# Two hand-kept instruction orders rewritten, and one gate load moved to another place in GpSimd's queue

## The reference

```
# block 1, per layer (adaLN scales from cond @ ada_w)
h = rmsnorm(x) * (1 + sc_m) + sh_m
proj = h @ w_in                       # 1024 -> 2824
out_a = sliding_window_attention(rope(norm(aq)), rope(norm(ak)), av)
out_b = rmsnorm(hgrn2_chunked(bq, log_f, bv)) * silu(bg)
out_c = rmsnorm(gated_delta_chunked(l2norm(cq), l2norm(ck), cv, beta, g)) * silu(cg)
x = x + gt_m * (concat(out_a, out_b, out_c) @ w_out)
x = x + gt_f * swiglu(rmsnorm(x) * (1 + sc_f) + sh_f)
# block 2, per layer
proj = x @ w_in_2                     # z, xbc, dt, dq, dk, dv, dg, cq, cg, gates
y_ssd  = ssd(forward + backward) * silu(z), rmsnorm
y_diff = rmsnorm(diff_attention(dq, dk, dv)) * silu(dg)
y_cross = attention(cq, mem @ w_mem_kv) * silu(cg)
merged = sum(gate_i * (y_i @ w_br_i))
x = layernorm(alpha * x + merged @ w_out_2)
```

## Time and profile before

| | |
|---|---|
| median of 3 runs | 3927.32 us (3926.3 to 3929.07) |
| the profiled execution | 3926.3 us, span 3923.8 us |
| TensorE busy | 3772.4 us, 96% of the span |
| VectorE busy | 2615.8 us, 67% |
| ScalarE busy | 1563.3 us, 40% |
| GpSimd busy | 181.5 us, 5% |
| granted TensorE clock, mean | 0.981 of full |

### The profile page before, as it was taken

One profiled execution on the slowest core, in us unless ns is written; L12 is line 12 of the kernel. 1 busy time (PEld: TensorE's weight loads), 2 busy tenths in 40 slices (PEclk: granted clock), 3 DMA queues, 4 the chain that ended last, 5 costly groups with the idle time before them and its releaser, 6 DMA issues.

```text
span 3923.8 us, 49406 instructions
## 1 busy us (share of the span) xinstructions
PE 3772.4 (96%) x19461; PEld 3094.3 (79%) x19461; DVE 2615.8 (67%) x4153; ACT 1563.3 (40%) x2633; POOL 181.5 (5%) x335
## 2 busy tenths in 40 slices
PE   7989999999999999999999999999999999999998
PEld 6769878888779788878887788678778877886786
DVE  6887455555785522457889753876668898437866
ACT  3453332234643422333443333554344433335542
POOL 0000000000000000000111000000001110000010
PEclk9999899999999899999999999999999999999999
DMA  7502256533212332334555232133244553331242
GB/s 239 181 22 76 81 169 211 190 115 97 68 39 65 111 97 83 105 113 132 157 164 161 70 99 81 63 120 132 74 152 141 156 169 97 92 91 60 71 151 106
DMA packets 226871, 451.59 MB, mean 115 GB/s; under 512 B 18560, under 2 KB 63648, under 8 KB 224592
## 3 DMA queue, kind: packets, MB, share of 16 engines
q1 hardware_dynamic: 197584, 335.12, 26.8%
q0 software_dynamic: 29056, 113.32, 9.1%
HBM read 412.45 MB, written 35.93 MB: 114 GB/s over the span
## 4 chain that ended last, share of the span: by engine, by line
PE 76%; DVE 15%; ACT 5%; DMA 2%; issue 2%; SPq 0%; DVEq 0%; POOL 0%; ACTq 0%; POOLq 0%
PE ps L605 59%; PE ps L148 11%; DVE arena L170 4%; PE ps L159 3%; DVE spl L170 3%; ACT arena L244 3%; DVE arena L185 3%; DVE sm L191 1%; PE ps L154 1%; DVE X L170 1%; ACT sph L244 1%; PE ps L900 1%; DVE arena L177 1%; DMA arena<-cumd 1%; DVE arena L221 1%
## 5 line engine op out<-in xcount | busy, mean ns | idle before, releaser
L170 DVE TENSOR_TENSOR spl<-ring,sph 128x1024 fp32r<-128x1024 f32 (+3 forms) x556 | 650.2, 1177 | 701.1 <-ACT sph L244 700.3
L244 ACT ACTIVATE sph<-ring 128x1024 fp32r<-128x1024 f32 (+3 forms) x556 | 558.7, 1019 | 723.7 <-PE ps L605 680.8
L605 PE MATMUL ps<-sph,HTh 128*128 128x512 f32 (+2 forms) x1632 | 636.0, 390 | 9.7 <-DVE HTl L170 5.0
L605 PE MATMUL ps<-spl,HTh 128*128 128x512 f32 (+2 forms) x1632 | 601.5, 369 | 0.0
L605 PE MATMUL ps<-sph,HTl 128*128 128x512 f32 (+2 forms) x1632 | 600.7, 368 | 0.0
L244 ACT ACTIVATE arena<-ps 128x512 f32<-128x512 f32 (+2 forms) x572 | 315.2, 563 | 675.1 <-PE ps L605 400.3
L605 PE MATMUL ps<-HTh,sph 128*128 128x512 f32 x1360 | 536.4, 394 | 0.3 <-DVE arena L170 0.3
L605 PE MATMUL ps<-HTh,spl 128*128 128x512 f32 x1360 | 529.6, 389 | 0.0
L605 PE MATMUL ps<-HTl,sph 128*128 128x512 f32 x1360 | 529.5, 389 | 0.0
L605 PE MATMUL ps<-sph 128*128 128x512 f32 x992 | 399.1, 402 | 4.8 <-DVE spl L170 4.8
L605 PE MATMUL ps<-sph,spl 128*128 128x512 f32 x992 | 389.0, 392 | 0.0
(11 more groups left out here) (228 smaller groups left out, 4919.5 us busy)
## 6 DMA issues: line engine op xcount, KB each, us to landing
ring<-in_w_in SPq DMA_DIRECT2D x264, 512.0 KB, 4.0
arena<-in_ada_w SPq DMA_DIRECT2D x88, 512.0 KB, 4.9
arena<-cumd POOLq DMA_DIRECT2D x128, 256.0 KB, 4.0
ring<-in_w_down SPq DMA_DIRECT2D x44, 512.0 KB, 3.7
ring<-in_w_gate SPq DMA_DIRECT2D x40, 512.0 KB, 3.8
ring<-in_w_up SPq DMA_DIRECT2D x40, 512.0 KB, 4.2
ring<-in_w_mem SPq DMA_DIRECT2D x32, 512.0 KB, 3.5
ring<-in_w_out SPq DMA_DIRECT2D x32, 512.0 KB, 3.7
```

What stands on the lines that cost most here:

```text
L170: self.e.tensor_tensor(o, a, b, op).then_inc(*self.done.up())
L244: self.e.activation(o, a, f, **kw).then_inc(*self.done.up())
L605: ins = pe.e.matmul(o, l, r, start=k0 == 0 and i == 0 and not b.pairs, stop=k0 + b.ks == b.kt and i == 3 * b.ks - 1 and (c0 > 0 or not b.p ...
```

## The change

The strings of ('mix', 0) and ('mix', 1) are replaced. Each has the same number of each letter as before, in another order; the strings of `proj` stay. And the load of gate half 1 goes from `pool_before` into `dnorm_pool`, to the first step of dnorm's second half, beside that of half 0 in the first.

```
 SCORES = {
     ('mix', 0):
-        "7MtMt5MtMt2Mt10M2a7Ma6MaMhMa5Mh2Mch2Mh2Mc4Mc5Mac3Ma7Mta3Mah4Ma7MaMa3McaMhca2Mh2Mhac4Mc2Mac2ga2gh3gah"
-        "gagagagag2agagagag2agag3a2g2agag2a2gmhgihihi2mihiMhMihiMihMihiMh2Mi2Mihihi2Mi4Mi2Mi2h3M2iMh2i2MhihMi"
-        "hMi2MhiMh2ihMih2Mh3MiM2iM2i2M3i2M2i3Mb22M",
+        "14Mt3MtM2t10MtM2a7Ma4Ma2MhMaMc2Mh3MhMh2Mc2Mc5Ma3Mca9Ma3Mah8Ma3Mc2MaMaMahMc2MaMahMc2Mc4Mc2gaha2gh3gah"
+        "a2gagagag2agagagag2agag2ag3a3g2a3gahmihtimhim2Mihi3MihiMi5M2hihi2Mih3MiMh2iM2iMihiMih2iMi2h2Mi2MhMihi"
+        "hMhihMh2iMihMh4MiM2iM2i2M2iMiM2i4Mb21M",
     ('mix', 1):
-        "26MaM3a5Ma2MhMhMa2M2aMa2M2ahaM2caMac7Mh4Mh5McMac2Ma2MaMa2MahcMaMhMhaMcMc2Mc2M3gh4gahga2ga2gaga2g2aga"
-        "gagag3agag3a3gmgih2i2mhi2MiMiMhMhiMhihiMh2MihM2ihihiM2ih3MihihMh3M2iMh3MhMiMhihiMiM2ihiMihMhi2M2iMih"
-        "i2M2i2MiM2iMb28M",
+        "24Ma7Ma2M2aMh2Ma2c2MhacMacM3aMhMhM3a2Ma7Mh4Mc4Mhac2MaMa3Maca2McMaMaMchMh4M2gh5gha2gag2a4gag2agag2aga"
+        "g2ag2ag2agm3gihimhim3Mhi2Mi2MhiMhihiMiMhihi3MiMhiMiMihMiMhi2h2MhMi3MhiMh2iM3ihihihiMhi2hMi2M2iM2i2M2"
+        "i2MiMiMi11Mb17M",
@@ def pool_before(p):
                 if which == 1:
-                    p.wait_ge(at["ds", l, 31, 1], *[at["stg", l, 28 + m] for m in range(4)])
-                    at["dgin", l, 1] = p.move(ld["dg"], DGb[1], Dg[:, :, 512:1024].rearrange("m p n -> p m n"))
                     p.wait_ge(at[("br", l, 0), "merged", 7], at[(("br", l, 0), 1), 3], *[at["stg", l, 32 + j] for j in range(8)])
                     at["cgin", l] = p.move(ld["cg"], OC, Cg.rearrange("m p n -> p m n"))
@@ def dnorm_pool(p, l):
             for nb in range(2):
+                p.wait_ge(at["ds", l, 16 * nb + 15, 1], *[at["stg", l, 24 + 4 * nb + m] for m in range(4)])
+                at["dgin", l, nb] = p.move(ld["dg"], DGb[nb], Dg[:, :, nb * 512:(nb + 1) * 512].rearrange("m p n -> p m n"))
                 if nb == 0:
-                    p.wait_ge(at["ds", l, 15, 1], *[at["stg", l, 24 + m] for m in range(4)])
-                    at["dgin", l, 0] = p.move(ld["dg"], DGb[0], Dg[:, :, 0:512].rearrange("m p n -> p m n"))
                     p.wait_ge(at["od_t", l, 15], at["mk_stored", l])
                     at["mkin", l] = p.move(ld["mk"], MK, KVd[l, :, 0:2048].rearrange("p (a b) -> p a b", a=4))
```

More of the change, by code:

```diff
@@ L46 @@
     ('mix', 0):
-        "7MtMt5MtMt2Mt10M2a7Ma6MaMhMa5Mh2Mch2Mh2Mc4Mc5Mac3Ma7Mta3Mah4Ma7MaMa3McaMhca2Mh2Mhac4Mc2Mac2ga2gh3gah"
-        "gagagagag2agagagag2agag3a2g2agag2a2gmhgihihi2mihiMhMihiMihMihiMh2Mi2Mihihi2Mi4Mi2Mi2h3M2iMh2i2MhihMi"
-        "hMi2MhiMh2ihMih2Mh3MiM2iM2i2M3i2M2i3Mb22M",
+        "14Mt3MtM2t10MtM2a7Ma4Ma2MhMaMc2Mh3MhMh2Mc2Mc5Ma3Mca9Ma3Mah8Ma3Mc2MaMaMahMc2MaMahMc2Mc4Mc2gaha2gh3gah"
+        "a2gagagag2agagagag2agag2ag3a3g2a3gahmihtimhim2Mihi3MihMi5M2hihi2Mih3MiMh2iM2iMihiMih2iMi2h2Mi2MhMihi"
+        "hMhihMh2iMihMh4MiM2iM2i2M2iMiM2i4Mb21M",
     ('mix', 1):
-        "26MaM3a5Ma2MhMhMa2M2aMa2M2ahaM2caMac7Mh4Mh5McMac2Ma2MaMa2MahcMaMhMhaMcMc2Mc2M3gh4gahga2ga2gaga2g2aga"
-        "gagag3agag3a3gmgih2i2mhi2MiMiMhMhiMhihiMh2MihM2ihihiM2ih3MihihMh3M2iMh3MhMiMhihiMiM2ihiMihMhi2M2iMih"
-        "i2M2i2MiM2iMb28M",
+        "24Ma7Ma2M2aMh2Ma2c2MhacMacM3aMhMhM3a2Ma7Mh4Mc4Mhac2MaMa3Maca2McMaMaMchMh4M2gh5gha2gag2a4gag2agag2aga"
+        "g2ag2ag2agm3gihimhim3Mhi2Mi2MhiMhihiMiMhihi3MiMhiMiMihMiMhi2h2MhMi3MhiMh2iM3ihihihiMhi2hMi2M2iM2i2M2"
+        "i2MiMiMi11Mb17M",
     ('proj', 0):
```

## The result

The changed kernel takes 3950.68 us (median of 4 runs, 3947.94 to 3954.68) against 3927.86 us, a ratio of 1.0064, 95% interval 1.0049 to 1.0080. It is slower by 23 us. The forecast was 3928.5 us, no change, with 3940 as the upper end of its range, and 0.16 for slower. It was wrong.

A forecast was written before the change was run, and what follows sets the result against it. TensorE, busy 3772.4 of 3923.8 us, was taken as the bound. Orders -2 -1 -1 -1.5 and load +4.2 +2.5 gave +1.2 on 3926.3, so 3927.5; with 1.0 for the median 3928.5 us, range 3915 to 3940.

The forecast's parts named there:

- Layer 1, first stretch: Stretch of mix layer 1 with projections: earlier convolution steps change the time by -1 us, between -2.6 and +1.
- the one that lost: Rival: eight close inverse steps in layer 1's third stretch wait 1.2 us each, 13 us more, about 3941 us; chance 0.14.
- The moved load: Last layer: half 1 lands late, VectorE waits 4.6 us, TensorE stops 4.2 us; hidden in layer 0, 0 for kvd.
- the term of 6.7: The load's share of the sum: 4.2 us of TensorE stop and 2.5 us of reduced clock in the last layer.
- The rival that the load is hidden: Half 1 lands before VectorE needs it in the last layer, only the orders count: 3921.8 us; chance 0.1.
- the estimate of 14.0 us: Time for 5.24 MB in one row by the skill page's figures, putting half 1's landing in the last layer just in time.
- The clock behind a stall: Reduced TensorE clock after the last layer's 4.2 us stop: 2.5 us lost, between 0 and 3.4.
- The other orders: New order in layer 0's first stretch -2 us, second stretches -1 (layer 0) and -1.5 (layer 1), third and fourth 0.
- second to fourth stretches of layer 1: mix layer 1 without main steps (-1.5 us), inverse with memory products (0), serial state pass (0).
- the wait of 6.16 us: TensorE's wait for VectorE in layer 0's first stretch, inside one h step; forecast to stay.
- the 7.03 us: TensorE's wait for VectorE at g11 in layer 1's second stretch; forecast to fall to about 5.
- its inputs are long ready: Claim that a24, 3.68 us long, placed before g11 in layer 1's second stretch, can run in TensorE's idle time there.

The follow-up runs named there:

- conv_only: The kernel before with only four convolution steps, c0 to c3 of mix layer 1, moved earlier: 3940.01 us, +12.7.
- h3_early: The kernel before with one step moved, h3 (decayed linear attention) of mix layer 1, seven main steps earlier: 3936.74 us, +6.7.
- front_old: The kernel before with the new string of mix layer 1 only from the first g step on: 3930.84 us against 3930.03.
- load_only: The kernel before with only the load of gate half 1 moved, both strings old: 3934.51 us against 3927.27.
- orders_only: The changed kernel with the load of gate half 1 back in its old place, both new strings kept: 3944.11 us, +16.8.
- mix1_only: The kernel before with only the string of mix layer 1 replaced by the new one: 3943.05 us, +15.8.
- load_mid: The kernel before with the load of gate half 1 issued between those of kvd and the four gd tiles: 3928.26 us against 3927.55.
- h3_c5: The kernel before with two steps of mix layer 1 moved earlier, h3 directly behind main step 41 and c5 behind c4: ratio 1.0017.

## Why the prediction was wrong, step by step

**The failed step is "Layer 1, first stretch".** It took -1 us, between -2.6 and +1, and the stretch lost 12.4. I bounded the gain by a row, TensorE's 2.6 us of idle time, and the loss by nothing: "may hold VectorE a little" has no row behind it. I looked at c3 and asked whether its own data would be there. The question that decides is who stands behind it. VectorE is busy 89.70 of 110 us there, the c steps are 10.5 us of work with no hurry, and moved up they stand ahead of a softmax and of low parts that TensorE waits for. The rows for it were in the trace of before. a8 came 11.9 us later against the opening product, and 10.5 for c0 to c3 and 2.9 for a4 (no longer done in an earlier idle time of VectorE), less VectorE's 0.77 and 0.60 us of idle time there, make 12.0. conv_only and h3_early show that such a move alone costs TensorE 8.2 and 4.2 us. None of the rivals had it: the one that lost put its loss into the close run i18 to i25, where front_old shows nothing.

**The moved load** was right in its mechanism and nearly in its size. Alone it has 4.63, 4.03 and about 1.7 us for the forecast's 4.6, 4.2 and 2.5, and +7.2 us for the term of 6.7. Half 1 landed 17.9 us after the issue of `cgd`, for the 18.6 worked out; that the wait of VectorE still came out at 4.6 is luck, for VectorE too was there 0.7 us sooner after that issue (13.3 us for 14.0). In layer 0 it was hidden, as forecast: no wait for it is in the trace. Nor was anything won for `kvd` in layer 0, where TensorE waits 2.35 us for 2.44. In the changed kernel the same load costs about 8 us, because half 1 landed 1.6 us later there; whether the orders have to do with that is open. The rival that the load is hidden, and with it the estimate of 14.0 us by the page "DMA: Bandwidth & Descriptors" of the Trainium skill (Anatomy of one DMA), is refuted: 17.9 and 19.5 us were measured, beside a weight load on another queue.

**The clock behind a stall.** Between 0 and 3.4 us was the range, 2.5 taken; 1.7 was read in load_only, and about 16 x 0.21 = 3.4 us in the changed kernel, whose window from 3768 to 3784 has 0.79:

```profile
3768.00:3784.00 16.00, 10.37 (x40) 8.38 (x39) 10.65 (x20) 0.00 (x0) 0.00 (x0) 0.79 0.01 4
```

The page "TensorE: Matmul & The Clock Gate" of the Trainium skill (HAM oscillation) says that waits for data re-throttle the array each time; both windows agree, with 0.86 and 0.79. The full 3.4 us that the prediction worked out with it came in the second and not in the first.

**The other orders.** For layer 0 and for the second to fourth stretches of layer 1 I counted -2, -1, -1.5 and 0. Measured are 1 us (orders_only less mix1_only) and 0.8 (front_old less the kernel before), both within noise. That they are near nothing was right; the gains of 4.5 us in all are not there to see. In layer 0 the wait of 6.16 us of the earlier trace rows is 6.72 in the changed kernel. In layer 1 the 7.03 us did not shrink in the way that was forecast. a24 does stand ahead of g11 now, but it can't run at once there, as "its inputs are long ready" had it: TensorE waits 3.95 us for VectorE in front of it, and again in front of the g steps, 0.56, 1.47 and 1.02 us, 7.0 us in all. TensorE of front_old:

```profile
1079.01 3.51 PE L148 MATMUL ps<-arena 128*64 128x512 f32 x4 [3.95 <-DVE arena L185]
```

What follows starts within 1 us of where it did, for VectorE's chain sets the end, as the prediction itself had said.

**The range** had 3940 as its upper end because every term that could lose had a bound of a few microseconds. One missing bound made it 11 us too narrow.

## What to carry to other kernels

Before a step is moved up in an in-order schedule, add up its work on each engine and ask for every instruction that it is put ahead of who needs that one and how late it may come; that the moved step's own data is ready says nothing. An engine at 80% has no free room if its work comes in bursts: here 4 us of work ahead of a weight tile cost 4 us. Late work isn't one account over the whole stretch. Part the order where the late engine has to wait for the other anyway (h4's products here) and count its work in each piece: a third convolution step between h4 and main step 60 cost 6 us, whether nothing or 4 us had been lost before it, and losses in two pieces added up. For a load, count the bytes in front of it in its queue from the first issue on, and give the first place to what is used first.

## What the runs showed that I had not expected

The same instructions in the same order did not take the same time in the fourth stretch of `mix` layer 0. Windows from 408 to 470 us of the kernel before, of load_mid and of conv_only, in which layer 0's order is the old one:

```profile
408.00:470.00 62.00, 60.48 (x371) 50.91 (x371) 23.02 (x55) 19.64 (x46) 1.59 (x3) 0.83 0.23 84
```
```profile
408.00:470.00 62.00, 60.98 (x338) 51.62 (x337) 20.60 (x50) 16.36 (x39) 1.59 (x3) 0.72 0.20 68
```

The earlier trace rows have 0.75; load_mid has 0.83 and conv_only 0.72, and 371 and 338 matmuls in 62 us for 347. TensorE is in between its two levels there and falls to the lower one more or less often from one execution to the next. That is several microseconds in a kernel whose runs spread from 3921 to 3934 us in one group, and why a single execution's span says less here than a distance between two instructions.

The wait for `kvd` in layer 0 is not fixed either: 2.44 us in the earlier trace rows, 2.35 in load_only, 3.74 in orders_only, 4.09 in conv_only, 2.08 in h3_early and 4.38 in h3_c5, though of these only load_only changes that layer's order of loads. What sets it was not tested.
